# Gathering the experts' tokens from a split of the normalized rows, in fp32r instead of fp32

## The chip, the cores and the metric

One Trainium2 chip, one of its cores. The metric is the time of one execution on the device in microseconds (us). Four engines work in parallel: TensorE (in the profile PE for its products and PEld for its weight loads), VectorE (DVE), ScalarE (ACT) and GpSimd (POOL). SyncE (SP) issues most transfers.

## The reference, cut to what matters

Two layers of attention and feed-forward over 256 tokens of 1024 numbers, and a second block behind them. The part that the change touches is the feed-forward of the second layer, a mixture of 8 experts of which each token takes two:

```python
def moe_swiglu(h, router, wg, wu, wd):
    logits = (h @ router).astype(jnp.float32)
    top_vals, top_idx = lax.top_k(logits, TOP_K)
    gates = jax.nn.softmax(top_vals, axis=-1)
    ...
    for e in range(N_EXPERTS):
        out = out + gate_e[..., e:e + 1] * swiglu(h, wg[e], wu[e], wd[e])
```

`h` is the normalized input: x divided by its root mean square, times a gain per column. D is 1024, the inner width 3584, all in float32.

## The kernel before, in words

Products that need float32's precision are made in one of two ways. In plain fp32, TensorE takes both operands as they are. In fp32r, an operand is first split: ScalarE makes a rounded copy (the high part), VectorE subtracts it from the original (the low part), and three fp32r products (high by high, high by low, low by high) add up in PSUM. All expert weights go the second way: for each half of a unit of gate and up weights ScalarE copies (line 1675, `unit_high`) and VectorE subtracts (line 2256, `A_parts`, called by `unit_low`), and the same for the down weights (lines 1705 and 2336).

If no expert has more than 128 tokens, which is so here, each expert works on its own tokens alone. The steps for expert e:

- `one_hot` (line 2352) makes `sel`, 256 tokens by 128 slots, with a one where a token has a slot.
- `gather(e)` on TensorE (line 949) multiplies the normalized rows `xn` (the stationary operand, 128 tokens by 128 columns at a time) with `sel` (the moving operand, 128 slots wide): 8 blocks of columns by 2 blocks of tokens, 16 products in fp32. They go to the PSUM banks 6 and 7.
- `dispatch` on VectorE (line 2360) applies the gain and writes `xgT`; ScalarE (line 1725, `rows_part`) and VectorE (line 2371) split it into `xgs`.
- 14 units of 256 inner columns: gate and up products against `xgs` (line 894, two halves of 12 products), the gated hidden rows turned (line 909), split (ACT line 1685, DVE line 2317) and multiplied with the down weights (line 924, 12 products).
- `scatter` (line 962) puts the result back on the tokens, out of `ye`, a split of the expert's output whose low half lies in `hTR`.

The gather for expert e + 1 is issued by expert e after its unit 12 of 0 to 13, behind two turns of `selg` (line 975). Only the gather of expert 0 stands alone, ahead of all units. There is one buffer each for a half of the split gate and up weights and for the down weights, so VectorE's and ScalarE's work for one half waits until TensorE has used the half before. Every engine runs its own list in order; semaphores tie the lists. In expert 0, ScalarE runs `before(n)` at the start of unit n and VectorE runs `after(n)` at its end; GpSimd at the same time makes gate rows (lines 1486 to 1495) for the second block.

`hTR` is an fp32r buffer of 2048 columns whose storage is that of `hT`, the turned input of this and the earlier layers. In the expert branch it holds the low half of `ye`, and at the very end of the last expert the high part of one block of down weights.

Of the kernel before, what the change touches and what calls it, by code (L numbers as in the profile page):

```python
# [21 lines left out]
F32R = mybir.dt.float32r  # L22
I32 = mybir.dt.int32
U32 = mybir.dt.uint32
ALU = mybir.AluOpType
ACT = mybir.ActivationFunctionType
# [106 lines left out]
def build(nc, t, out, AT1, N1, AT2, N2):  # L133
    ctx = ExitStack()
    with ctx:
        def sb(name, shape, dt=F32):
            return ctx.enter_context(nc.sbuf_tensor(name, shape, dt))

        def sem(name):
            return ctx.enter_context(nc.semaphore(name))  # L140
# [7 lines left out]
        with nc.sbuf_tensor("hcTR", [P, KC, SEQ], F32R) as hcTR:  # L148
            pass
        hcT = sb("hcT", [P, KC, SEQ])  # L150
        xn = sb("xn", [P, TILES, D])
        with nc.sbuf_tensor("ringL", [P, 2, KC, BW], F32R) as ringL:
            pass
# [41 lines left out]
        As = sb("As", [P, 2, 2, KC // 2, BW], F32R)  # L195
        Bs = sb("Bs", [P, FB // P, 2, D], F32R)
        hds = sb("hds", [P, 2, 2, FB // P, P], F32R)
        f32 = lambda v: v.bitcast(F32)

        def ar(off, *shape):  # L200
            n = int(np.prod(shape))
            assert off + n <= AR_N, (off, n)
            v = arena[:, off:off + n]
            if len(shape) == 1:
                return v
            if len(shape) == 2:
                return v.rearrange("p (a b) -> p a b", a=shape[0])
            return v.rearrange("p (a b c) -> p a b c", a=shape[0], b=shape[1])
# [22 lines left out]
            return by_rows(xs[:, 0, :, :] if p["name"] == "ff0x" else hTR[:, :, :]), by_rows(ringH[:, b % 2, :, :])  # L231

        xgT = ar(0, KC, P)
        ye = arenaR[:, 1024:1024 + D], hTR[:, 0:4, :].rearrange("p k n -> p (k n)")
        sel = ar(2048, TILES, P)
        selg = ar(2304, TILES, P)
        selT = arenaR[:, 2560:2560 + TILES * P].rearrange("p (t s) -> p t s", t=TILES)
        chosen = ar(2816, TILES, NE)
# [93 lines left out]
        gates_open = sem("gates_open")  # L332
        y_mixed = sem("y_mixed")
        y_high = sem("y_high")
        xh_high, xh_low, z_first, i_lin, u_high, u_split = (sem(n) for n in ("xh_high", "xh_low", "z_first", "i_lin", "u_high", "u_split"))
        o_scaled, ot_tp, ot_hi, ot_lo = (sem(n) for n in ("o_scaled", "ot_tp", "ot_hi", "ot_lo"))
        wo_std, x_mixed, pn_plain, fin_std, x_out = (sem(n) for n in ("wo_std", "x_mixed", "pn_plain", "fin_std", "x_out"))
# [359 lines left out]
        def _(pe):  # L697
# [242 lines left out]
            def gather(e):  # L940

                pe.wait_ge(sel_ready, e + 1)
                if not isinstance(e, int) or e >= 2:
                    pe.wait_ge(added, 2 * e - 2)
                for half in range(2):
                    for k in range(4):
                        for tt in range(TILES):
                            o = (4 * half + k) * P
                            last = mm(ps[:, 6 + half, k * P:(k + 1) * P], xn[:, tt, o:o + P], sel[:, tt, :], start=tt == 0, stop=tt == TILES - 1)  # L949
                    last.then_inc(gathered, 1)  # L950

            def scatter(e, tt):
# [547 lines left out]
        def _(act):  # L1500
# [232 lines left out]
            def expert(e):  # L1733

                first, final = isinstance(e, int) and e == 0, isinstance(e, int) and e == NE - 1

                def before(n):
                    if n == 2 and not first:
                        keep_y(e - 1)

                def body(i, u, last):
                    if isinstance(i, int):
                        before(2 * i + u)
                    lead = first and isinstance(i, int) and i == 0
                    nxt = (i + 1, 0) if u else (i, 1)
                    if not lead:
                        part_high(e, i - 1, u, 1)
                    unit_high(e, *nxt, 0)
                    if last and not final:
                        rows_part(e + 1, 0)  # L1750
                    if u == 0:
                        gate_silu(e, i, 1)
                    unit_high(e, *nxt, 1)
                    if last and not final:
                        rows_part(e + 1, 1)
                    if last and final:
                        down_high(e, i, 0, down_home(ph["moe"], ph["moe"]["b"])[0], 0)
                        part_high(e, i, 0, 1)
                        part_high(e, i, 1, 1, 3)
                        down_high(e, i, 1, None, 2)  # L1760
                    elif u:
                        down_high(e, i, 0)
                    elif not lead:
                        down_high(e, i - 1, 1)
                blocks(act, NB1, body, 2)
                if final:
                    keep_y(e)
# [390 lines left out]
        def _(dve):  # L2158
# [214 lines left out]
            def expert(e):  # L2373

                first, final = isinstance(e, int) and e == 0, isinstance(e, int) and e == NE - 1

                def after(n):
                    if n in (2, 3) and not first:
                        add(e - 1, n - 2)
                    if n == 3:  # L2380
                        if not first:
                            dve.wait_ge(selg_tp, e)
                        one_hot(e, 2 * e + 2, True)
                        if not final:
                            dve.wait_ge(gathered, 2 * e + 2)
                            one_hot(e + 1, 2 * e + 3, False)
                    if n == NB1 - 2 and not final:
                        dispatch(e + 1)

                def body(i, u, last):  # L2390
                    lead = first and isinstance(i, int) and i == 0
                    nxt = (i + 1, 0) if u else (i, 1)
                    if isinstance(i, int) and i == 1 and u == 0 and not first:
                        y_low(e - 1)
                    if last:
                        gate_sums(e)
                    if not lead:
                        part_low(e, i - 1, u, 1)
                    unit_low(e, *nxt, 0)
                    if last and not final:  # L2400
                        rows_part(e + 1, 0)
                    if u:
                        gate_times_up(e, i, 1)
                    unit_low(e, *nxt, 1)
                    if last and not final:
                        rows_part(e + 1, 1)
                    if last and final:
                        down_low(e, i, 0, down_home(ph["moe"], ph["moe"]["b"]))
                        part_low(e, i, 0, 1)
                        part_low(e, i, 1, 1, 3)  # L2410
                        down_low(e, i, 1)
                    elif u:
                        down_low(e, i, 0)
                    elif not lead:
                        down_low(e, i - 1, 1)
                    if isinstance(i, int):
                        after(2 * i + u)
                blocks(dve, NB1, body, 2)
                if final:
                    y_low(e)  # L2420
                    dve.wait_ge(down_done, e * (2 * NB1) + (ph["moe"]["s"] + 2 * NB1))
# [615 lines left out]
```

## Time and profile before

| | |
|---|---|
| median of 3 runs | 2683.97 us (2683.48 to 2686.52) |
| the profiled execution | 2684.65 us |
| its span, first to last instruction | 2682.9 us |
| TensorE busy / weight loads busy | 2556.0 us (95%) / 2030.1 us (76%) |
| VectorE / ScalarE / GpSimd busy | 1819.1 (68%) / 1452.3 (54%) / 53.2 us (2%) |
| line 949, the gathers | 256 product records, 31.5 us busy |
| granted TensorE clock, mean | 0.972 of full speed |

The profiled execution is 1.75 us over its span and 0.7 us over the median of the runs. Product records overlap: each lasts from the entry of its first column to the end of its last, and the next one starts before that. What a product costs is therefore the distance between starts, and in a row that merges n of them it is the row's length, less one record's, divided by n - 1. A busy share near 100% says that products followed one another, not that the array worked at its peak.

### The profile page before, as it was taken

What the parts mean: (1) busy time and instruction counts of PE and PEld (TensorE: products, weight loads), DVE (VectorE), ACT (ScalarE), POOL (GpSimd) and SP (SyncE); (2) the same over time, 40 slices, a digit from 0 to 9 for tenths busy, and PEclk for the clock granted to TensorE, in tenths of its full rate; (3) what the DMA queues carried; (4) which work ended last, traced back from release to release, by engine and by line L of the source; (5) the groups of instructions that cost most, each with busy time, mean ns of one, the idle gap of its engine ahead of it and who ended that gap; (6) DMA issues with size and microseconds to landing.
All of it is one profiled execution on the core that took longest, in us unless ns stands there. A gap on an engine that the chain in (4) does not pass through costs nothing.

```text
span 2682.9 us, 33560 instructions
## 1 busy us (share of the span) xinstructions
PE 2556.0 (95%) x11949; PEld 2030.1 (76%) x11949; DVE 1819.1 (68%) x1778; ACT 1452.3 (54%) x1613; POOL 53.2 (2%) x40
## 2 busy tenths in 40 slices
PE   7899998888999999999999998999999999998998
PEld 6568887656878787878888886888884687776787
DVE  6554445548898988888888886545443475776544
ACT  4554434535677777777677675445432243466443
POOL 0000000016000000000000000000000000000000
PEclk9999998879999999999999998999999999999999
DMA  6865542749999999999999996556543343435552
GB/s 215 294 216 187 185 164 81 249 158 332 370 330 347 353 345 355 347 353 346 354 343 357 342 336 222 184 179 195 180 167 108 92 154 116 139 96 176 194 186 70
DMA packets 327743, 631.65 MB, mean 235 GB/s; under 512 B 14089, under 2 KB 112937, under 8 KB 327465
## 3 DMA queue, kind: packets, MB, share of 16 engines
q1 hardware_dynamic: 326792, 627.35, 67.4%
q0 software_dynamic: 864, 3.15, 0.3%
q8 instruction: 55, 0.90, 0.1%
q14 instruction: 32, 0.25, 0.0%
HBM read 629.40 MB, written 1.05 MB: 235 GB/s over the span
## 4 chain that ended last, share of the span: by engine, by line
PE 83%; DVE 8%; ACT 4%; issue 3%; DMA 1%; SPq 0%; DVEq 0%; ACTq 0%
PE ps L820 19%; PE ps L894 18%; PE ps L924 10%; PE ps L849 9%; PE ps L1285 6%; PE ps L754 5%; PE ps L1312 2%; DVE As L2256 2%; PE ps L1027 1%; PE ps L1217 1%; PE ps L949 1%; ACT As L1675 1%; PE ps L833 1%; PE ps L1276 1%; PE ps L909 1%
## 5 line engine op out<-in xcount | busy, mean ns | idle before, releaser
L2256 DVE TENSOR_TENSOR As<-ringA,As 128x2048 fp32r<-128x2048 f32 x318 | 735.8, 2316 | 224.5 <-ACT As L1594 129.5
L894 PE MATMUL ps<-As,xgs 128*128 128x512 f32 x2688 | 660.6, 395 | 9.8 <-DVE As L2256 6.7
L894 PEld LDWEIGHTS ps<-As,xgs 128*128 128x128 f32 x2688 | 494.8, 188 | 117.1 <-issue 7.1
L1675 ACT ACTIVATE As<-ringA 128x2048 fp32r<-128x2048 f32 x224 | 428.7, 1914 | 31.7 <-PE ps L894 30.2
L820 PE MATMUL ps<-As,xs 128*128 128x512 f32 x1632 | 392.4, 397 | 9.4 <-issue 5.4
L820 PEld LDWEIGHTS ps<-As,xs 128*128 128x128 f32 x1632 | 306.7, 190 | 76.1 <-issue 5.8
L924 PE MATMUL ps<-Bs,hds 128*128 128x512 f32 x1332 | 322.6, 391 | 10.5 <-DVE hds L2317 10.2
L924 PEld LDWEIGHTS ps<-Bs,hds 128*128 128x128 f32 x1332 | 248.6, 188 | 68.7 <-issue 15.2
L2336 DVE TENSOR_TENSOR Bs<-ringB,Bs 128x2048 fp32r<-128x2048 f32 x111 | 255.7, 2304 | 10.1 <-ACT Bs L1705 8.6
L1705 ACT ACTIVATE Bs<-ringB 128x2048 fp32r<-128x2048 f32 x111 | 213.1, 1920 | 69.9 <-PE ps L924 69.9
L849 PE MATMUL ps<-Bs,hds 128*128 128x512 f32 x1056 | 247.8, 390 | 0.0
L849 PEld LDWEIGHTS ps<-Bs,hds 128*128 128x128 f32 x1056 | 198.0, 188 | 41.9
L1594 ACT ACTIVATE As<-ringA 128x2048 fp32r<-128x2048 f32 x94 | 179.7, 1912 | 17.4 <-DMA ringA<-in_dense_w_up 10.1
L2300 DVE TENSOR_TENSOR Bs<-ringB,Bs 128x2048 fp32r<-128x2048 f32 x44 | 100.8, 2292 | 119.7 <-ACT Bs L1648 119.7
L1648 ACT ACTIVATE Bs<-ringB 128x2048 fp32r<-128x2048 f32 x44 | 84.3, 1916 | 135.4 <-PE ps L849 135.4
L2226 DVE TENSOR_TENSOR ringL<-ringA,ringH 128x2048 fp32r<-128x2048 f32 x42 | 96.1, 2290 | 57.4 <-ACT ringH L1574 57.1
L754 PE MATMUL ps<-As,xs 128*128 128x512 f32 (+1 forms) x384 | 119.0, 394 | 9.0 <-DVE ringL L2226 6.1
L1685 ACT ACTIVATE hds<-ps 128x256 fp32r<-128x256 f32 x112 | 43.1, 384 | 154.8 <-PE ps L909 153.6
L1615 ACT ACTIVATE hds<-ps 128x256 fp32r<-128x256 f32 x94 | 31.3, 382 | 170.8 <-PE ps L833 162.7
L1574 ACT ACTIVATE ringH<-ringA 128x2048 fp32r<-128x2048 f32 x42 | 80.1, 1910 | 79.2 <-PE ps L1285 57.7
L820 PE MATMUL ps<-As,hcTR 128*128 128x512 f32 x352 | 111.6, 398 | 0.0
L1636 ACT ACTIVATE sg<-ps 128x256 f32<-128x256 f32 x94 | 36.1, 385 | 126.8 <-PE ps L820 125.8
(380 smaller groups left out, 3214.6 us busy)
## 6 DMA issues: line engine op xcount, KB each, us to landing
ringA<-in_moe_w_gate SPq DMA_DIRECT2D x112, 1024.0 KB, 5.2
ringA<-in_moe_w_up SPq DMA_DIRECT2D x112, 1024.0 KB, 5.3
ringB<-in_moe_w_down SPq DMA_DIRECT2D x112, 1024.0 KB, 5.5
ringA<-in_w_ff_in SPq DMA_DIRECT2D x132, 512.0 KB, 4.8
ringA<-in_w_in SPq DMA_DIRECT2D x56, 1024.0 KB, 5.4
ringA<-in_w_ada SPq DMA_DIRECT2D x36, 1024.0 KB, 6.8
ringB<-in_w_ff_out SPq DMA_DIRECT2D x33, 1024.0 KB, 5.0
ringA<-in_dense_w_gate SPq DMA_DIRECT2D x28, 512.0 KB, 3.7
```

The source lines that it names most:

```text
L754: m = mm(ps[:, 4 + 2 * (n % 2) + tt, 0:cols], xs[:, l, k, tt * P:(tt + 1) * P], w, start=k == 0 and m_ == 0, stop=k == KC - 1 and m_ == 2)
L820: m = mm(ps[:, bank, :], lhs(l, tt, k), As[:, h, r, k % 4, :], start=k == 0 and n == 0, stop=k == KC - 1 and n == 2)
L849: m = mm(ps[:, 4 + 2 * tt + half, :], hds[:, buf, l, q, :], w[:, half * 512:(half + 1) * 512], start=first and q == 0 and n == 0, stop=q = ...
L894: m = mm(ps[:, bank, :], lhs(l, tt, k), As[:, h, r, k % 4, :], start=k == 0 and n == 0, stop=k == KC - 1 and n == 2)
L924: m = mm(ps[:, 4 + 2 * tt + half, :], hds[:, u if T == 1 else tt, l, q, :], (Bs[:, q, r, :] if weights is None else weights[r][:, q, :])[: ...
L1285: m = mm(dst, lhs[l][:, k, tt * P:(tt + 1) * P], w[q], start=k == 0 and m_ == 0, stop=k == KC - 1 and m_ == 2)
L1594: A(As[:, h, 0, :, :], ringA[:, (p["a"] + u) % 2, 4 * h:4 * h + 4, :], ACT.Copy).then_inc(A_high, 1)
L1675: A(As[:, h, 0, :, :], ringA[:, (p["a"] + u) % 2, 4 * h:4 * h + 4, :], ACT.Copy).then_inc(A_high, 1)
L1705: A(Bs[:, :, 0, :] if dst is None else dst, ringB[:, b0 % 2, :, :], ACT.Copy).then_inc(B_high, 1)
L2256: V.tensor_tensor(As[:, h, 1, :, :], ringA[:, (p["a"] + u) % 2, 4 * h:4 * h + 4, :], f32(As[:, h, 0, :, :]), ALU.subtract).then_inc(A_spli ...
L2300: V.tensor_tensor(Bs[:, :, 1, :], ringB[:, (p["b"] + u) % 2, :, :], f32(Bs[:, :, 0, :]), ALU.subtract).then_inc(B_low, 1)
L2336: V.tensor_tensor(lo, ringB[:, (p["b"] + u) % 2, :, :], f32(hi), ALU.subtract).then_inc(B_low, 1)
```

## The change

Once, during expert 0, the normalized rows are split. ScalarE writes a rounded copy of all of `xn` (128 by 2048) into `hTR`, at the start of unit 2, after the gather of expert 0 has read `xn`. VectorE subtracts it from `xn` in place, into `xnR`, an fp32r name of the same storage, at the end of unit 2. The gathers of experts 1 to 7 then make two fp32r products (high by `sel`, low by `sel`) for each one in fp32, so 32 products of 128 columns; `sel` is written in fp32r. The gather of expert 0 stays in fp32 and reads `sel` under its fp32 name. Since `hTR` is now taken for all of the experts, the low half of `ye` gets a buffer of its own, `yl`. Two semaphores are new.

```diff
+        with nc.sbuf_tensor("xnR", [P, TILES, D], F32R) as xnR:
+            pass
         xn = sb("xn", [P, TILES, D])
...
+        yl = sb("yl", [P, D], F32R)
...
-        ye = arenaR[:, 1024:1024 + D], hTR[:, 0:4, :].rearrange("p k n -> p (k n)")
-        sel = ar(2048, TILES, P)
+        ye = arenaR[:, 1024:1024 + D], yl[:, :]
+        x_split = hTR[:, :, :].rearrange("p k n -> p (k n)").rearrange("p (t n) -> p t n", t=TILES), xnR[:, :, :]
+        sel = arenaR[:, 2048:2048 + TILES * P].rearrange("p (t s) -> p t s", t=TILES)
...
+        xn_high, xn_split = sem("xn_high"), sem("xn_split")
... (TensorE, gather)
+                whole = isinstance(e, int) and e == 0
+                if not whole:
+                    pe.wait_ge(xn_split, 1)
                 for half in range(2):
                     for k in range(4):
+                        o = (4 * half + k) * P
                         for tt in range(TILES):
-                            o = (4 * half + k) * P
-                            last = mm(ps[:, 6 + half, k * P:(k + 1) * P], xn[:, tt, o:o + P], sel[:, tt, :], start=tt == 0, stop=tt == TILES - 1)
+                            if whole:
+                                last = mm(ps[:, 6 + half, k * P:(k + 1) * P], xn[:, tt, o:o + P], f32(sel[:, tt, :]), start=tt == 0, stop=tt == TILES - 1)
+                                continue
+                            for q in range(2):
+                                last = mm(ps[:, 6 + half, k * P:(k + 1) * P], x_split[q][:, tt, o:o + P], sel[:, tt, :], start=tt == 0 and q == 0, stop=tt == TILES - 1 and q == 1)
                     last.then_inc(gathered, 1)
... (ScalarE, expert, before(n))
+                    if n == 2 and first:
+                        act.wait_ge(gathered, 2)
+                        A(x_split[0], xn[:, :, :], ACT.Copy).then_inc(xn_high, 1)
... (VectorE, expert, after(n))
+                    if n == 2 and first:
+                        dve.wait_ge(xn_high, 1)
+                        V.tensor_tensor(x_split[1], xn[:, :, :], f32(x_split[0]), ALU.subtract).then_inc(xn_split, 1)
```

## Rows read from the trace of the kernel before

**Rows 1.** The page's first two parts: busy time, and the granted clock by slices.
```profile
PE 2556.0 (95%) x11949; PEld 2030.1 (76%) x11949; DVE 1819.1 (68%) x1778; ACT 1452.3 (54%) x1613; POOL 53.2 (2%) x40
...
PEclk9999998879999999999999998999999999999999
```

**Rows 2.** The page's chain of work that ended last, by engine.
```profile
PE 83%; DVE 8%; ACT 4%; issue 3%; DMA 1%; SPq 0%; DVEq 0%; ACTq 0%
```

**Rows 3.** The source line of the gathers: record durations in ns, and waits.
```profile
L949 PEld LDWEIGHTS ps<-arena,xn x256: 190/192/333, 605.6 to 1489.5; 128*128 128x128 f32 x128
L949 PE MATMUL ps<-arena,xn x256: 274/275/582, 605.6 to 1489.7; 128*128 128x128 f32 x128
its engine sat idle before it (us, times) until:
  DVE arena L2352: 8.5, 2
```

**Rows 4.** Timeline, all engines, around expert 1's gather: start, length, what, idle before.
```profile
728.33 0.38 PE L975 MATMUL ps<-c,arena 128*128 128x128 f32 x2
728.44 3.65 PEld L949 LDWEIGHTS ps<-arena,xn 128*128 128x128 f32 x32
728.55 3.74 PE L949 MATMUL ps<-arena,xn 128*128 128x128 f32 x32
728.59 1.91 ACT L1705 ACTIVATE Bs<-ringB 128x2048 fp32r<-128x2048 f32 x1 [0.34 <-PE ps L924]
730.53 2.29 DVE L2336 TENSOR_TENSOR Bs<-ringB,Bs 128x2048 fp32r<-128x2048 f32 x1
...
732.04 3.01 PE L894 MATMUL ps<-As,xgs 128*128 128x512 f32 x12
732.74 1.28 DVE L2360 TENSOR_TENSOR arena<-ps,vcol 128x512 f32<-128x512 f32 x2
...
740.60 2.93 PE L894 MATMUL ps<-As,xgs 128*128 128x512 f32 x12
```

**Rows 5.** Timeline of TensorE: narrow fp32 products, two or eight records a row.
```profile
500.11 0.39 PE L1077 MATMUL ps<-arena 128*128 128x64 f32 x2
500.33 0.39 PE L1078 MATMUL ps<-arena 128*128 128x64 f32 x2
500.56 0.39 PE L1079 MATMUL ps<-arena 128*128 128x64 f32 x2
...
504.85 1.05 PE L1009 MATMUL ps<-c,arow 128*128 128x2 f32 x8
```

**Rows 6.** Timeline of TensorE: fp32r products of 256 columns, first and last of 67.
```profile
2130.08 0.28 PE L1312 MATMUL ps<-hcTR,ringH 128*128 128x256 f32 x1
...
2138.00 0.28 PE L1312 MATMUL ps<-hcTR,ringH 128*128 128x256 f32 x1
```

**Rows 7.** Source lines: record durations, ns min/median/max.
```profile
L1009 PE MATMUL ps<-c,arow x96: 223/251/374, 83.3 to 541.9; 128*128 128x2 f32 x96
...
L1027 PEld LDWEIGHTS ps<-ringA,cT x288: 106/110/178, 74.8 to 595.0; 128*32 128x32 f32 x144
...
L894 PEld LDWEIGHTS ps<-As,xgs x2688: 186/188/192, 612.9 to 1616.9; 128*128 128x128 f32 x192
```

**Rows 8.** TensorE's groups of products by form: the fp32r lines' widths and means.
```profile
L894 PE MATMUL ps<-As,xgs 128*128 128x512 f32 x2688 | 660.6, 395 | 9.8 <-DVE As L2256 6.7 <-DVE xgs L2371 2.6
...
L1312 PE MATMUL ps<-hTR,ringH 128*128 128x256 f32 x192 | 55.1, 287 | 0.0
```

**Rows 9.** Stretches: length, busy PE, PEld, DVE, ACT, POOL (records), clock, DMA, GB/s.
```profile
644.89:675.00 30.11, 26.75 (x115) 20.82 (x115) 30.04 (x24) 18.48 (x13) 13.57 (x6) 1.00 0.99 369
675.00:728.30 53.30, 53.30 (x241) 43.78 (x240) 46.32 (x29) 40.09 (x29) 0.00 (x0) 1.00 1.02 379
728.30:744.00 15.70, 15.52 (x88) 13.06 (x86) 13.23 (x13) 9.06 (x8) 0.00 (x0) 1.00 0.78 281
...
857.90:874.00 16.10, 15.95 (x74) 12.73 (x73) 13.58 (x14) 9.75 (x10) 0.00 (x0) 1.00 0.78 269
```

**Rows 10.** Timeline, ACT, DVE and PE around expert 0's unit 2.
```profile
628.55 1.90 ACT L1705 ACTIVATE Bs<-ringB 128x2048 fp32r<-128x2048 f32 x1
...
631.37 0.39 ACT L1685 ACTIVATE hds<-ps 128x256 fp32r<-128x256 f32 x1 [0.92 <-issue]
631.65 1.91 ACT L1675 ACTIVATE As<-ringA 128x2048 fp32r<-128x2048 f32 x1
...
634.49 0.41 DVE L2317 TENSOR_TENSOR hds<-ps,hds 128x256 fp32r<-128x256 f32 x1
...
634.82 2.28 DVE L2256 TENSOR_TENSOR As<-ringA,As 128x2048 fp32r<-128x2048 f32 x1
...
641.44 3.12 DVE L2336 TENSOR_TENSOR Bs<-ringB,Bs 128x2048 fp32r<-128x2048 f32 x1
...
644.48 0.41 DVE L2317 TENSOR_TENSOR hds<-ps,hds 128x256 fp32r<-128x256 f32 x1
...
644.95 3.01 PE L924 MATMUL ps<-Bs,hds 128*128 128x512 f32 x12 [0.36 <-DVE hds L2317]
...
647.61 3.89 DVE L2256 TENSOR_TENSOR As<-ringA,As 128x2048 fp32r<-128x2048 f32 x1
```

**Rows 11.** The chain of work in 612 to 676 us, by line.
```profile
by line: DVE As L2256 43.2%; PE ps L894 25.0%; issue 12.0%; ACT As L1675 9.0%; DVE Bs L2336 3.6%; DVE hh L2329 2.0%; DVE xgs L2371 1.8%; PE ps L924 1.4%; DVE arena L2350 0.9%; DVE hds L2317 0.5%; DVE small L2346 0.3%; DVE small L2345 0.2%; 
```

## The prediction

> **What bounds the kernel now.** I read the page's busy shares first: TensorE is busy for 95% of the span at nearly the full clock, VectorE for 68% [rows 1], and the chain that ended last lies on TensorE for 83% of its length and on VectorE for 8% [rows 2]. The gathers are TensorE's work, so a shorter or longer gather should show in the total, unless VectorE stands right behind it. I therefore read three places. The first is the line of the gathers: 256 records for 8 gathers of 16 products, so a product in fp32 is two records, each with a weight load of its own [rows 3]. The second is the timeline of one gather in the middle of the run. There TensorE goes without a gap from the turns of `selg` into the gather and from it into the next unit [rows 4]; 32 records take 3.74 us, one lasts 0.275, so their starts are (3.74 - 0.275) / 31 = 0.112 us apart and a gather is 32 x 0.112 = 3.58 us of TensorE's time. The stretches around two such boundaries show TensorE idle for only 15.70 - 15.52 = 0.18 and 16.10 - 15.95 = 0.15 us [rows 9]. The third is expert 0, where the split is put. From 644.89 to 675.00 us VectorE is busy 30.04 of 30.11 us and TensorE idle 3.36; behind it, to 728.30, TensorE is never idle and VectorE has 7 of 53 us free [rows 9]. The chain through 612 to 676 us goes mostly over VectorE [rows 11]. So the gathers lie where TensorE sets the pace, and the new subtraction lies where VectorE does.
>
> **Part 1: the seven gathers of experts 1 to 7.** The records go from 32 with fp32 operands to 32 with fp32r operands. What sets 0.112 us? It could be the columns that pass, or the weight load ahead of each record. Narrower fp32 products answer it. With 64 columns instead of 128 the starts of three pairs are 500.11, 500.33 and 500.56, so 0.11 us per record; with 2 columns it is (1.05 - 0.25) / 7 = 0.114 [rows 5], one such record being 0.25 [rows 7]. Half the columns, or almost none, change nothing: below 128 columns the spacing is that of the loads of 128 weight columns. The loads' own records agree: 32 columns take 110 ns, 128 take 192 [rows 3, 7], so 0.85 ns per column and 109 ns for 128, the rest being latency.
>
> An fp32r product still loads 128 weight columns, and its load record is 188 ns [rows 7] against 192 for fp32 [rows 3], so I take it to be as long. The number of loads does not fall either: it was 2 per product for 16 products, it is 1 per product for 32. So 32 x 0.112 = 3.58 us against 3.58 us, and part 1 gives 0. The columns that pass may well halve, but they are hidden behind the loads.
>
> No row shows an fp32r product of under 256 columns: the narrowest are those of line 1312 [rows 8]. They start (2138.00 - 2130.08) / 66 = 0.120 us apart [rows 6]. From them come the bounds. Below: if the load did not count, half of 0.120 for half the columns, 0.060, so 32 x 0.060 = 1.92 us, 1.66 less per gather and 11.6 us less for seven. Close above: 0.120 as it stands, 32 x 0.008 = 0.26 us more per gather, 1.8 us for seven. Far above: if a product this narrow is carried out in the four passes of fp32, it is two records of 0.112, 32 x 0.224 = 7.17 us, 3.58 more per gather and 25.1 us for seven. I take 0, because the load's duration is the one thing that a row shows for both kinds. The added wait for `xn_split` was satisfied some 80 us before the first gather that asks for it: nothing.
>
> Two rules of the Trainium skill say otherwise. Its page FP8 and Floating Point Precision, section TensorE Precision Notes, has true fp32 as four passes through the array and the reduced kind as one of truncated values; by it a gather's passes fall from 64 to 32, and the sum would be the rival of the halved gather below. The rows agree on the passes of wide products and do not show them to count in narrow ones. Its page TensorE: Matmul & The Clock Gate, section Back-to-back issue gap, gives a stream of pairs of load and product with 128 columns some 81 ns each; by that figure seven gathers would shrink by 7 x 32 x 0.031 = 7 us, an estimate from that page. This trace shows no pair under 110 ns, which is why I do not use it.
>
> **Part 2: VectorE's subtraction, 128 by 2048, at the end of unit 2 of expert 0.** The same form costs 2.28 us on line 2256 undisturbed, and 3.89 when GpSimd works beside it [rows 10]. It goes in after line 2336 (641.44 + 3.12 = 644.56) and ahead of the split of the hidden rows at 644.48, for which TensorE already waits 0.36 us ahead of its down products at 644.95 [rows 10]. Behind the subtraction are that split, then both halves of the next unit's weights. VectorE has no free time up to 675 us in which to catch up [rows 9]. After it TensorE cannot make the lost time good, since it is never idle there. So it comes out of the end in full: +2.3 us. The bounds are 0 (if the wait is made good by work of GpSimd's that no longer falls on VectorE's) and 3.9 (if GpSimd slows it).
>
> **Part 3: ScalarE's copy, 128 by 2048, at the start of unit 2.** It costs 1.9 us, as line 1675 does. Its place is between 628.55 + 1.90 = 630.45 and the copy of the hidden rows at 631.37 [rows 10]: 0.92 us of it is free time. The hidden rows' copy and line 1675 move by 1.0 us, the latter to 631.65 + 1.0 + 1.91 = 634.56. VectorE comes to its subtraction for this copy at 634.82 anyway, and to the hidden rows at 634.49 [rows 10]. So the cover is VectorE's lag and the cost is 0, with 0.26 us to spare; without the cover it is up to 1.0 us. Its wait for the gather of expert 0 was met at 611 us.
>
> **Part 4: what moves.** The low half of `ye` in its own buffer and `sel` in fp32r leave the same instructions on VectorE with the same shapes: 0. No transfer is added or moved past a queue.
>
> **The sum** against the profiled execution's 2684.65 us is 0 + 2.3 + 0 + 0 = 2687.0 us. That execution is 0.7 us above the median of the runs, so the forecast for the median is 2683.97 + 2.3 = 2686.3 us, 0.09% more.
>
> **The rivals.**
>
> *A narrow fp32r product takes all four passes.* For it: this kernel has not one fp32r product under 256 columns, and nothing in the trace says that the single pass holds below that. Against it: the records of 512 and 256 columns last 395 and 287 ns [rows 8], in step with one pass of the columns, with no sign of a change on the way down. Time: seven gathers 25.1 longer, less the 0.15 to 0.18 us that TensorE idles at each boundary now (7 x 0.17 = 1.2), plus the split's 2.3: 2683.97 + 26.2 = 2710.2 us, slower by 1.0%. It decides as soon as the spacing passes 0.13 us: 7 x 32 x 0.014 = 3.1 us and the split together reach the 5.4 us that are 0.2%.
>
> *The gather is halved.* For it: half the passes. Against it: the loads. It needs an fp32r load of under 0.06 us, and the load's record gives no hint of that. VectorE also sets a limit: its instruction ahead of the dispatch ends at 730.53 + 2.29 = 732.82 whatever the gather does [rows 4], and the next expert's first products at 740.60 wait for rows that come from it. I allow 0.25 us lost per boundary. Time: 2683.97 - 11.6 + 1.8 + 2.3 = 2676.5 us, faster by 0.28%.
>
> *The split is hidden too, or costs double.* Same gathers, 2684.0 to 2689.7 us (3.9 for a slowed subtraction and 1.8 for a spacing of 0.120). The upper end is just past 0.2%.
>
> **How the numbers follow.** A measurement of this kernel tells about 0.2%, 5.4 us, from no change. The gather as long as before: 0.52, of which 0.03 lie above 2689.4. Four passes: 0.34, because nothing in the trace covers widths under 256 columns. Halved: 0.10. Something between the last two, or unforeseen: 0.04. The likeliest case is the first, 2686.3 us, its own range 2683.5 to 2690. To leave out no more than 2 in 10 the range must take in the case of four passes: 2681 to 2713 us; the halved gather falls outside. Chances: faster 0.11, within 0.2% 0.51, slower 0.38.
>
> **What would show it.** In the profile after, the gathers of experts 1 to 7 are 32 records each, on hTR and xn: if their starts are 0.11 us apart, part 1 holds; 0.06 is the halved gather; 64 records, or starts over 0.2 apart, the four passes. The product records should be shorter than 275 ns while the spacing stays, if the columns halve behind the loads. TensorE's first unit after the first gather should start 3.5 us after its start (now 728.55 to 732.04). In expert 0 TensorE should wait about 2.6 us for VectorE's line 2317 near 645 us, and be free of waits from about 677 us. The prediction is wrong if the weight load in fp32r is not what its record suggests, or if VectorE makes the 2.3 us good before 675.

## The result, and the profile after

| | before | after |
|---|---|---|
| median of 14 runs each | 2683.35 us (2679.23 to 2687.08) | 2690.98 us (2682.97 to 2696.61) |
| ratio, 95% interval | | 1.0026 (1.0018 to 1.0034) |
| profiled execution, span | 2682.9 us | 2688.9 us |

The changed kernel is slower by 0.26% by the ratio of all runs (7.0 us), just past the 0.2% that I had set as the bound of what can be told; the interval, 0.18 to 0.34%, reaches a little below that bound. The forecast was +2.3 us; it became +7.6 us in the medians and +6.0 in the two spans. The median lies in the stated range of 2681 to 2713 us, but above the 2683.5 to 2690 that I gave the likeliest case.

The page of the changed kernel, busy time and chain by engine, beside [rows 1, 2]:

```profile
PE 2556.0 (95%) x11949; PEld 2029.6 (75%) x11949; DVE 1823.0 (68%) x1779; ACT 1453.7 (54%) x1614; POOL 54.4 (2%) x40
...
PE 84%; DVE 7%; ACT 4%; issue 3%; DMA 1%; SPq 0%; DVEq 0%; ACTq 0%
```

TensorE is busy for the same 2556.0 us with the same 11949 records. So, summed over the whole execution, the 6.0 us of the spans are idle time of TensorE's and not longer products. VectorE has one instruction and 3.9 us more, ScalarE one instruction and 1.4 us more.

**The gathers.** The source line of the fp32r gathers, the half of its records with the high part (number, durations in ns min/median/max, first and last start), beside [rows 3]:

```profile
L961 PEld LDWEIGHTS ps<-arenaR,hTR x112: 190/192/192, 734.4 to 1495.3; 128*128 128x128 f32 x112
L961 PE MATMUL ps<-arenaR,hTR x112: 273/275/305, 734.4 to 1495.3; 128*128 128x128 f32 x112
```

And TensorE's timeline around the first of them (start, length, line, output<-inputs), beside [rows 4]:

```profile
734.39 0.30 PE L961 MATMUL ps<-arenaR,hTR 128*128 128x128 f32 x1
734.53 0.28 PE L961 MATMUL ps<-arenaR,xnR 128*128 128x128 f32 x1
...
737.88 0.27 PE L961 MATMUL ps<-arenaR,xnR 128*128 128x128 f32 x1
737.99 0.68 PE L899 MATMUL ps<-As,xgs 128*128 128x512 f32 x2
```

With as many for the low part, which last as long, these are 224 records, 32 for each of seven gathers. Their starts are (737.88 - 734.39) / 31 = 0.113 us apart, and the next unit's first product starts 3.60 us after the gather's, where before it was 732.04 - 728.55 = 3.49 [rows 4] (0.03 of the 0.11 more lies between the first two records). The loads last 192 ns as before. The product records last 275 ns too: they did not get shorter.

**Where the loss lies.** Stretches of the changed kernel: from the gather of expert 0 to that of expert 1, the last part of it, most of the six experts that follow, and two short stretches that come up below (columns as in [rows 9]):

```profile
604.75:734.39 129.64, 113.39 (x501) 91.46 (x501) 107.80 (x67) 80.33 (x58) 42.42 (x17) 0.96 0.91 328
...
677.00:734.30 57.30, 57.30 (x260) 47.00 (x259) 49.98 (x32) 42.59 (x32) 0.00 (x0) 1.00 1.01 369
760.00:1480.00 720.00, 710.96 (x3262) 581.33 (x3261) 638.55 (x457) 513.70 (x377) 0.00 (x0) 1.00 0.96 350
...
660.00:668.00 8.00, 5.86 (x18) 4.73 (x19) 6.37 (x6) 0.97 (x1) 5.00 (x2) 0.62 0.64 228
...
649.06:653.48 4.42, 3.40 (x15) 2.48 (x14) 4.42 (x4) 1.91 (x1) 0.61 (x1) 1.00 0.72 231
```

The same stretches of the kernel before, whose rows were not shown ahead of the prediction:

```profile
605.63:728.55 122.92, 112.29 (x501) 90.21 (x502) 104.97 (x66) 78.70 (x57) 41.26 (x17) 0.99 0.95 350
760.00:1480.00 720.00, 711.15 (x3261) 581.26 (x3260) 638.15 (x458) 513.26 (x377) 0.00 (x0) 1.00 0.96 350
...
649.94:657.50 7.56, 5.85 (x26) 4.31 (x25) 7.49 (x12) 4.63 (x5) 0.60 (x1) 1.00 1.04 393
```

Expert 0 takes 129.64 us instead of 122.92, which is 6.7 us more, for 501 product records in both. 5.6 of them are idle time of TensorE's (16.25 against 10.63) and 1.1 are longer products (113.39 against 112.29), at a mean clock of 0.96 against 0.99. Since the first gather starts 0.9 us earlier than before (604.75 against 605.63), 5.8 of the 6.7 reach the second gather's start (734.39 against 728.55), nearly all of the spans' 6.0. From 760 to 1480 us nothing differs, and from 677.00 on TensorE is busy without a break, so nothing that expert 0 lost is regained there. From the last gather's last record to the end of the span it is 1193.5 us after (2688.9 - 1495.4) and 1193.2 before (2682.9 - 1489.7).

**The chain of events in expert 0.** Timeline of the changed kernel, all engines, the rows that matter:

```profile
629.84 1.89 ACT L1754 ACTIVATE hTR<-xn 128x2048 fp32r<-128x2048 f32 x1
...
634.29 2.28 DVE L2271 TENSOR_TENSOR As<-ringA,As 128x2048 fp32r<-128x2048 f32 x1
...
643.95 2.28 DVE L2395 TENSOR_TENSOR xnR<-xn,hTR 128x2048 fp32r<-128x2048 f32 x1
...
645.99 2.49 POOL L1507 TENSOR_TENSOR gateG<-gateG,arow 128x1024 f32<-128x1024 f32 x1 [2.37 <-DMA arow<-in_norm_g]
646.15 0.41 DVE L2332 TENSOR_TENSOR hds<-ps,hds 128x256 fp32r<-128x256 f32 x1
646.48 4.13 DVE L2271 TENSOR_TENSOR As<-ringA,As 128x2048 fp32r<-128x2048 f32 x1
...
646.62 3.04 PE L929 MATMUL ps<-Bs,hds 128*128 128x512 f32 x12 [2.57 <-DVE hds L2332]
649.06 0.61 POOL L1498 DMA_DIRECT2D arow<-in_b_ada  x1 [0.59 <-POOL gateG L1507]
...
653.48 4.37 POOL L1501 TENSOR_TENSOR gateG<-gateG,arow 128x1024 f32<-128x1024 f32 x1 [3.81 <-DMA arow<-in_b_ada]
...
655.54 2.33 DVE L2360 COPY small<-slots 128x2 f32<-128x2 f32 x1
...
657.98 1.90 DVE L2365 TENSOR_SCALAR arena<-c,small 128x128 f32<-128x128 f32 x2
...
658.74 2.78 POOL L1504 TENSOR_SCALAR gateG<-gateG 128x1024 f32<-128x1024 f32 x1
659.80 0.16 DVE L2360 COPY small<-slots 128x2 f32<-128x2 f32 x1
...
660.06 1.61 DVE L2367 TENSOR_SCALAR arenaR<-c,small 128x128 fp32r<-128x128 f32 x2
661.60 0.41 DVE L2332 TENSOR_TENSOR hds<-ps,hds 128x256 fp32r<-128x256 f32 x1
...
662.14 4.80 PE L929 MATMUL ps<-Bs,hds 128*128 128x512 f32 x12 [5.46 <-DVE hds L2332]
666.77 2.89 PE L899 MATMUL ps<-As,xgs 128*128 128x512 f32 x12
```

The one-hots of unit 3 of the kernel before, its timeline, for comparison:

```profile
649.94 0.60 POOL L1486 DMA_DIRECT2D arow<-in_b_ada  x1 [0.59 <-POOL gateG L1495]
...
653.63 0.15 DVE L2345 COPY small<-slots 128x2 f32<-128x2 f32 x1
...
653.89 0.60 DVE L2350 TENSOR_SCALAR arena<-c,small 128x128 f32<-128x128 f32 x2
...
655.07 0.42 DVE L2317 TENSOR_TENSOR hds<-ps,hds 128x256 fp32r<-128x256 f32 x1
...
655.62 3.01 PE L924 MATMUL ps<-Bs,hds 128*128 128x512 f32 x12 [1.05 <-DVE hds L2317]
657.53 2.42 POOL L1489 TENSOR_TENSOR gateG<-gateG,arow 128x1024 f32<-128x1024 f32 x1 [6.98 <-DMA arow<-in_b_ada]
```

The reader is to see three things in the changed kernel. The subtraction takes 2.28 us and starts right behind the down weights; the hidden rows' split comes 2.2 us after it, and TensorE waits 2.57 us. That is the forecast. Then come the eight small instructions that make the one-hots (`selg` and `sel`, two copies and two comparisons each). From the first of them at 655.54 to the hidden rows' split behind them at 661.60 it is 6.06 us, where before it was 655.07 - 653.63 = 1.44. The first of them copies 128 by 2 numbers, needs 0.15 us before and takes 2.33 here: it starts inside GpSimd's addition and ends at 657.87, with it (653.48 + 4.37 = 657.85). The two pairs of comparisons are stretched from 0.60 and 0.48 to 1.90 and 1.61. Last, TensorE waits 5.46 us for the hidden rows behind them (1.05 before), and the 12 products after that wait take 666.77 - 662.14 = 4.63 us of TensorE's time instead of some 2.85 (655.62 to 658.47 before). In the stretch around them, 660 to 668 us, the granted clock is 0.62 on average, between the full 2.4 GHz and the lower level of 1.2.

Counted from the first gather, the hidden rows of unit 3 are split 56.85 us after it instead of 49.44, so 7.4 later: 0.35 from ahead of the subtraction, 2.2 the subtraction, 0.24 between, 4.6 the one-hots. The 0.35 are not from ScalarE's copy: the first products of expert 0 are late by as much (612.43 - 604.75 = 7.68 against 612.96 - 605.63 = 7.33 before). The slow products bring it to 9.2. By the next gather it is 6.7: TensorE waits no more from 666.77 us on, where before it still had three waits for VectorE, 1.6 us in all of the 2.5 regained.

### The profile page after: what moved, and what is told of

It is laid out like the page before. It is cut to its first block, busy times and chain, and to the rows that moved or that the text cites. A ratio compares the mean times of both kernels' runs of the same rounds, so it can differ in the third digit from the quotient of the medians.

```text
span 2688.9 us, 33569 instructions
## 1 busy us (share of the span) xinstructions
PE 2556.0 (95%) x11949; PEld 2029.6 (75%) x11949; DVE 1823.0 (68%) x1779; ACT 1453.7 (54%) x1614; POOL 54.4 (2%) x40
## 3 DMA queue, kind: packets, MB, share of 16 engines
HBM read 629.40 MB, written 1.05 MB: 234 GB/s over the span
## 4 chain that ended last, share of the span: by engine, by line
PE 84%; DVE 7%; ACT 4%; issue 3%; DMA 1%; SPq 0%; DVEq 0%; ACTq 0%
PE ps L825 19%; PE ps L899 18%; PE ps L929 10%; PE ps L854 9%; PE ps L1297 6%; PE ps L759 5%; PE ps L1324 2%; DVE As L2271 2%; PE ps L1039 1%; PE ps L1229 1%; PE ps L961 1%; ACT As L1687 1%; PE ps L838 1%; PE ps L914 1%; PE ps L1288 1%
## 5 line engine op out<-in xcount | busy, mean ns | idle before, releaser
L2351 DVE TENSOR_TENSOR Bs<-ringB,Bs 128x2048 fp32r<-128x2048 f32 x111 | 255.0, 2297 | 12.8 <-ACT Bs L1717 11.3
```

The source lines that it names most:

```text
L2351: V.tensor_tensor(lo, ringB[:, (p["b"] + u) % 2, :, :], f32(hi), ALU.subtract).then_inc(B_low, 1)
```

## The experiments

Gather 0 and gather 1 below are the first starts of the gathers of experts 0 and 1; the one-hots' time is from the first small copy of unit 3 to the hidden rows' split. All are from one profiled execution each. Expert 0 does not start at the same time in all of them, and where it starts early (e2, e5) it is also longer, so both columns have to be read, the start of gather 1 and the distance.

| kernel | subtraction | gather 0 | gather 1 | apart | one-hots |
|---|---|---|---|---|---|
| before | none | 605.63 | 728.55 | 122.9 | 1.44 |
| after | unit 2 | 604.75 | 734.39 | 129.6 | 6.06 |
| e1 | unit 2 | 605.89 | 735.20 | 129.3 | 3.16 |
| e4 | unit 2 | 604.15 | 733.80 | 129.7 | 6.06 |
| e9 | unit 2 | 604.75 | 734.27 | 129.5 | 6.05 |
| e10 | unit 2 | 604.63 | 734.37 | 129.7 | 6.06 |
| e3 | unit 3, after the one-hots | 604.53 | 732.59 | 128.1 | 1.4 (and 2.2 the subtraction) |
| e6 | unit 8 | 604.04 | 728.88 | 124.8 | 1.44 |
| e5 | units 5 to 8, in quarters | 597.86 | 727.39 | 129.5 | 6.05 |
| e2 | none | 599.78 | 729.19 | 129.4 | 1.44 |
| e7 | none, GpSimd later | 601.58 | 717.53 | 116.0 | 1.46 |
| e8 | unit 2, GpSimd later | 599.98 | 717.34 | 117.4 | 1.45 |
| e11 | none, GpSimd later | 605.35 | 721.21 | 115.9 | 1.45 |
| e12 | unit 2, GpSimd later | 599.30 | 716.51 | 117.2 | 1.45 |

| kernel | median us (runs) | before, same chip | ratio (95%) |
|---|---|---|---|
| e1 | 2687.83 (9) | 2681.98 (27) | 1.0024 (1.0014 to 1.0034) |
| e2 | 2681.28 (11) | 2681.98 | 0.9995 (0.9985 to 1.0004) |
| e3 | 2687.43 (12) | 2681.98 | 1.0015 (1.0004 to 1.0025) |
| e4 | 2675.04 (6) | 2681.98 | 0.9973 (0.9961 to 0.9984) |
| e5 | 2684.99 (12) | 2683.58 (34) | 1.0004 (0.9995 to 1.0012) |
| e6 | 2687.06 (12) | 2683.58 | 1.0013 (1.0003 to 1.0024) |
| e7 | 2681.20 (12) | 2683.58 | 0.9990 (0.9981 to 0.9999) |
| e8 | 2677.74 (11) | 2683.58 | 0.9984 (0.9971 to 0.9996) |
| e9 | 2690.78 (1) | 2683.23 (19) | a single run |
| e10 | 2690.58 (1) | 2683.23 | a single run |
| e11 | 2674.13 (8) | 2683.23 | 0.9965 (0.9954 to 0.9976) |
| e12 | 2675.93 (12) | 2683.23 | 0.9975 (0.9966 to 0.9984) |

The ratio is taken over all runs and not from the two medians, so the two can differ by a microsecond or two: e3 is 5.5 us over in the medians and 4.0 by its ratio.

### The split without the fp32r gathers (e1)

The gathers are fp32 again and read the high part alone; the low part is left out.

```diff
-for q in range(2):
-    last = mm(ps[...], x_split[q][:, tt, o:o + P], sel[:, tt, :], start=tt == 0 and q == 0, stop=tt == TILES - 1 and q == 1)
+last = mm(ps[...], f32(x_split[0][:, tt, o:o + P]), f32(sel[:, tt, :]), start=tt == 0, stop=tt == TILES - 1)
```

> The split as in the changed kernel, but the gathers of experts 1 to 7 are 16 fp32 products again, read from the rounded high part alone (the low part is left out of the result). Theory 1 (the whole loss is the split in expert 0; 32 narrow fp32r products cost what 32 fp32 records did): as slow as the changed kernel, some 2690 us, 6 to 7 us over before. Rival (part of the loss is in the fp32r gathers): between before and the changed kernel, under 2687 us.

Timeline of this kernel, expert 0 and the first fp32 gather:

```profile
654.27 4.52 DVE L2350 TENSOR_TENSOR Bs<-ringB,Bs 128x2048 fp32r<-128x2048 f32 x1
658.72 0.99 DVE L2359 COPY small<-slots 128x2 f32<-128x2 f32 x1
...
662.43 5.24 PE L929 MATMUL ps<-Bs,hds 128*128 128x512 f32 x12 [4.82 <-DVE hds L2331]
...
735.20 3.74 PE L960 MATMUL ps<-arenaR,hTR 128*128 128x128 f32 x32
```

The ratio is that of the change, and gather 1 is as late. So, within the intervals, the whole loss comes with the split and none with the gathers. Here GpSimd's addition meets the down weights' subtraction (4.52 us instead of 2.28) and then its multiplication two of the small copies (0.99 and 1.04).

### The gathers and the copy without the subtraction (e2)

```diff
-pe.wait_ge(xn_split, 1)
+pe.wait_ge(xn_high, 1)
...
-last = mm(..., x_split[q][:, tt, o:o + P], sel[:, tt, :], ...)
+last = mm(..., x_split[0][:, tt, o:o + P], sel[:, tt, :], ...)
...
-if n == 2 and first:
-    dve.wait_ge(xn_high, 1)
-    V.tensor_tensor(x_split[1], xn[:, :, :], f32(x_split[0]), ALU.subtract).then_inc(xn_split, 1)
```

> The fp32r gathers with 32 narrow products and ScalarE's copy stay; VectorE's subtraction is gone, and both products of a pair read the high part (the low part is left out and the high one counts twice). Theory 1: the time of before, 2683 us, with 0.112 us between the gathers' starts, ScalarE's copy hidden. Rival (the copy or the gathers cost): 2686 us or more.

The time is that of before within the interval (4.0 us less to 1.1 more). 32 fp32r products for a gather and ScalarE's copy cost nothing that these runs can tell: the loss is VectorE's one instruction and what follows from it. The low part is left out here, and the high one counts twice. The profiled expert 0 of this run is 129.4 us long without any subtraction, but it began 6 us early, its one-hots took 1.44 us, and it reaches gather 1 at 729.19, as before; this is taken up under what stays open.

### Half the products (e4)

```diff
-for q in range(2):
-    last = mm(ps[...], x_split[q][:, tt, o:o + P], sel[:, tt, :], start=tt == 0 and q == 0, stop=tt == TILES - 1 and q == 1)
+last = mm(ps[...], x_split[0][:, tt, o:o + P], sel[:, tt, :], start=tt == 0, stop=tt == TILES - 1)
```

> As the changed kernel, but the gathers of experts 1 to 7 make only the high product of each pair, 16 fp32r products (the low part is left out). Theory 2 (a record costs its weight load, 0.112 us, whatever passes): each gather 16 x 0.112 = 1.8 us shorter, 12.5 us less for seven, 10 to 12 us under the changed kernel after what VectorE takes back at the boundaries. Rival (the boundaries are set by VectorE, and a shorter gather only turns into a wait): under 5 us less.

Timeline of TensorE at the first of these gathers:

```profile
733.80 1.98 PE L960 MATMUL ps<-arenaR,hTR 128*128 128x128 f32 x16
735.62 1.60 PE L899 MATMUL ps<-As,xgs 128*128 128x512 f32 x6
```

(1.98 - 0.275) / 15 = 0.114 us a record, and the next unit starts 1.82 us after the gather instead of 3.60. It is 12.8 us under e1, which has the same split and ran on the same chip; 7 x 16 x 0.112 = 12.5. So the gathers lie wholly on the path, and what counts there is the number of records. Had fp32r halved a record's time, as one rival has it, about as much would have come off the changed kernel's time.

### 64 and 256 columns in each product (e9, e10)

```diff
-last = mm(ps[:, 6 + half, k * P:(k + 1) * P], x_split[q][:, tt, o:o + P], sel[:, tt, :], ...)
+last = mm(ps[:, 6 + half, k * P:k * P + 64], x_split[q][:, tt, o:o + P], sel[:, tt, 0:64], ...)                       # e9
+last = mm(ps[:, 6 + half, (k // 2) * SEQ:(k // 2 + 1) * SEQ], x_split[q][:, tt, o:o + P], sel[...] as 256 columns, ...)  # e10
```

> As the changed kernel, but in the gathers of experts 1 to 7 each fp32r product takes only the first 64 slots of the selection (the other half of the gathered rows is left as it was). Theory 2 (the load of 128 weight columns sets the pace of a narrow fp32r product): starts 0.112 us apart as with 128 columns. Rival (the columns that pass set it): about 0.06 us apart.

> As the changed kernel, but in the gathers of experts 1 to 7 each fp32r product takes 256 columns, both tiles of the selection side by side, and two blocks share one place in PSUM (the gathered rows are a mixture). Theory 2: starts 0.12 us apart, as in the second block's products of 256 columns, so twice the columns for 7% more time. Rival (the columns set it): 0.22 us apart.

With 64 columns, the products of the high part by the source line, and the first and the last product of the first gather in the timeline:

```profile
L961 PE MATMUL ps<-arenaR,hTR x112: 276/277/339, 734.3 to 1496.7; 128*128 128x64 f32 x112
...
734.27 0.28 PE L961 MATMUL ps<-arenaR,hTR 128*128 128x64 f32 x1
...
737.78 0.40 PE L961 MATMUL ps<-arenaR,xnR 128*128 128x64 f32 x1
```

The same with 256:

```profile
L961 PE MATMUL ps<-arenaR,hTR x112: 279/281/366, 734.4 to 1497.0; 128*128 128x256 f32 x112
...
734.37 0.37 PE L961 MATMUL ps<-arenaR,hTR 128*128 128x256 f32 x1
...
738.13 0.28 PE L961 MATMUL ps<-arenaR,xnR 128*128 128x256 f32 x1
```

(737.78 - 734.27) / 31 = 0.113 us and (738.13 - 734.37) / 31 = 0.121. The loads last 192 and 188 ns. Half the columns change nothing and twice the columns add 7%. One run each gave 2690.78 and 2690.58 us; the changed kernel's median is 2690.98. So from 64 to 128 columns it is not the columns that set the pace but what a record costs besides, its weight load among it, and 256 columns cover that nearly evenly. That it is the load itself, and not some fixed cost of a record, is argued from the length of the load records ahead of the prediction; no run had products this narrow with fewer than 128 weight columns.

### The subtraction behind the one-hots (e3)

```diff
-(at the end of n == 2)
+(at the end of n == 3, after one_hot(e + 1, 2 * e + 3, False))
 dve.wait_ge(xn_high, 1)
 V.tensor_tensor(x_split[1], xn[:, :, :], f32(x_split[0]), ALU.subtract).then_inc(xn_split, 1)
```

> The subtraction moves from the end of unit 2 to the end of unit 3, behind the small one-hot instructions of that unit, which then keep their place between GpSimd's. Theory 1a (some 4 of the 6 us came because the late one-hots met GpSimd's addition and were held up, and TensorE's clock fell in the long wait): 2 to 3.5 us over before. Rival 1b (any 2.3 us of VectorE's work added in this phase costs 6): 6 us over before again. The long wait of TensorE for VectorE near 660 us should be about 3 us, not 5.5.

Timeline, VectorE and TensorE:

```profile
654.38 2.29 DVE L2404 TENSOR_TENSOR xnR<-xn,hTR 128x2048 fp32r<-128x2048 f32 x1
...
657.14 3.00 PE L929 MATMUL ps<-Bs,hds 128*128 128x512 f32 x12 [3.25 <-DVE hds L2332]
...
668.97 4.59 PE L929 MATMUL ps<-Bs,hds 128*128 128x512 f32 x12 [1.79 <-DVE hds L2332]
```

The one-hots, from 652.94, escape (0.16 us the first copy), as the order was meant to make them. But in this execution the loss is only moved: TensorE waits 1.79 us more a unit later, and those products again run at a low clock (4.59 us for 12). That wait follows a subtraction for the down weights that took 4.48 us beside GpSimd, at 664.02. The ratio, 1.0015, lies between the two theories, its interval (1.1 to 6.7 us) takes in both, and the median, 2687.43, is not to be told from e1's 2687.83. So e3 doesn't show that the one-hots alone make the excess.

### The split later: in quarters, or whole in unit 8 (e5, e6)

```diff
-if n == 2 and first:
+if 5 <= n <= 8 and first:        # e5: one quarter of 512 columns each; e6: if n == 8 and first:
...
-pe.wait_ge(xn_split, 1)
+pe.wait_ge(xn_split, 4)          # e5 only
...
-blocks(dve, NB1, body, 2)
+blocks(dve, NB1, body, 5 if first else 2)   # ScalarE's the same
```

> The split in four pieces of 128 by 512, one in each of the units 5 to 8 of expert 0, where GpSimd has finished and TensorE sets the pace; VectorE and ScalarE have units 0 to 9 of expert 0 written out for it. Theory 1 (the loss is where VectorE sets the pace): each 0.68 us fits into VectorE's free 1.1 us per unit, so the time of before, within 1 us. Rival (VectorE's free time cannot be used, since the single buffers tie it to TensorE): 2 to 3 us over before.

> The split in one piece in unit 8 of expert 0 (VectorE and ScalarE have units 0 to 9 written out). Theory 1: 2.3 us at once are more than the slack of one unit, so TensorE waits once, 0.5 to 1.5 us, and the time is 0.5 to 1.5 us over before, far under the changed kernel. Rival (a subtraction costs its full length or more wherever it stands): 2.3 us or more over before.

The quarters' source line in e5, and a row of the timeline of its unit 3, where no part of the split has run yet:

```profile
L2398 DVE TENSOR_TENSOR xnR<-xn,hTR x4: 684/684/685, 672.6 to 697.9; 128x512 fp32r<-128x512 f32 x4
...
647.62 2.33 DVE L2362 COPY small<-slots 128x2 f32<-128x2 f32 x1
```

The timeline of e6, TensorE behind the subtraction at 697.83:

```profile
700.58 3.01 PE L929 MATMUL ps<-Bs,hds 128*128 128x512 f32 x12 [1.17 <-DVE hds L2332]
```

In quarters the split is not to be told from nothing (1.0004). Whole, past GpSimd's work, it makes TensorE wait 1.17 us, and the profiled expert 0 is 1.9 us longer than before's. The median says +3.5, with an interval from 0.8 to 6.4 us; the profile accounts for about half of that. So the wait is the one that was expected, while the time is nearer to the rival's 2.3 us or more, which this experiment does not rule out. And e5 shows that the collision of one-hots and GpSimd needs no split: its expert 0 started 8 us early, its one-hots met GpSimd by themselves, and TensorE waited 5.44 us behind them.

### GpSimd's work moved behind the experts (e7, e8, e11, e12)

```diff
 pool.wait_ge(spread_copied, units_before(NADA))
+pool.wait_ge(x_ready, XR["moe"])                     # e7 on the kernel before, e8 on the changed one
+pool.wait_ge(down_done, ph["ff0c"]["s"] + 2 * 3)     # e11 on the kernel before, e12 on the changed one
```

> The kernel before with one wait added on GpSimd: its gate rows are made after the last expert instead of during expert 0. Theory 3 (GpSimd holds up VectorE in expert 0): VectorE's subtractions there take 2.3 us instead of up to 3.9, TensorE idles less between 613 and 675 us, and the time is 3 to 7 us under before. Rival (TensorE's waits there come from the pipeline's filling, and GpSimd's rows are then late or disturb the next phase): no change, or slower.

> The changed kernel with GpSimd's gate rows made after the last expert. Theory 1a and 3 (the extra 4 us are the meeting of the one-hots with GpSimd, and without it the subtraction costs at most its own 2.3 us): at most 2.3 us over the kernel before with the same wait, and at or under before. Rival 1b (the loss has nothing to do with GpSimd): again 6 us over the kernel before with the same wait.

> The kernel before, with GpSimd's gate rows made from the third unit of the feed-forward behind the experts on, where VectorE is half idle, not at its very start. Theory 3 (expert 0 gets 6 to 7 us shorter without GpSimd; with the rows right behind the experts part of it was lost again in the final normalization): 5 to 8 us under before. Rival (GpSimd disturbs VectorE as much there and TensorE waits for it): no more than the 2 to 4 us of the wait placed at the experts' end.

> The changed kernel with GpSimd's gate rows in the same place. Theory 1a: the split costs what its subtraction does, 1 to 2.5 us over the kernel before with the same placement. Rival 1b: 6 us over it.

The wait of e7 and e8 holds GpSimd's gate rows back until the last expert is done, that of e11 and e12 until the third unit of the feed-forward behind it. The timeline of e12, the changed kernel with GpSimd idle in expert 0:

```profile
636.75 0.50 PE L929 MATMUL ps<-Bs,hds 128*128 128x512 f32 x1 [0.94 <-DVE hds L2333]
...
644.03 0.16 DVE L2361 COPY small<-slots 128x2 f32<-128x2 f32 x1
```

Stretches of e11 behind the experts:

```profile
1640.00:1800.00 160.00, 160.00 (x722) 131.71 (x721) 92.13 (x82) 74.03 (x84) 41.02 (x18) 0.99 0.58 192
```

With GpSimd away from it, expert 0 is 7.1 us shorter without the split (e11, 115.9) and 12.4 shorter with it (e12, 117.2), and e7 and e8 give nearly the same (116.0 and 117.4). The split then lengthens the profiled expert 0 by 1.4 us in both pairs, instead of 6.7. The medians do not resolve so little: e12 is 1.8 us over e11, e8 is 3.5 us under e7, and in both pairs the intervals overlap. They do say that the 7.6 us are gone. In the profiles e8 and e12 also begin expert 0 earlier than e7 and e11, by 1.6 and 6.0 us, which no run explains.

At the first later place (e7) the 7 us came back behind the experts: from the last gather's last record to the end it took 1200.3 us against 1193.2 (1195.5 in e8), and the median is only 2.4 us under before, less than the 3 to 7 expected. At the second place GpSimd's 41 us lie in a stretch in which TensorE is busy 160.00 of 160.00 us and VectorE only 92. e11, the kernel before with one more wait, has the lowest median of the versions that leave nothing out: 0.35% under before, 9.1 us, a little more than the 5 to 8 expected. Its profiled execution, 2681.07 us, was the longest of its eight, with 1958.1 us from gather 1 to the end against before's 1954.4 and e12's 1953.2; where it lost these four was not followed up.

## Why the prediction was right in its parts and short in its sum

**Part 1 (0) held.** The columns do not set the pace: it is 0.113 us a record for 64 and 128 of them, 0.121 for 256. From gather 1's start to the last record of the last gather it is 761.0 us (734.39 to 1495.4), before 761.2 (728.55 to 1489.7). Neither four passes (64 records or 0.224 us) nor a halved gather appeared, and e2 finds no cost in the median. One guess about what would show it failed: the product records did not shorten. A record of 64, 128 or 256 columns lasts 277, 275 and 281 ns, so the length of a short record says nothing of its columns; the distance between starts does.

**Part 3 (0) held.** The copy runs at 629.84, the hidden rows' copy follows, and VectorE's subtraction for the next weights comes at 634.29 without a wait; the 0.35 us by which expert 0 is late there were lost before the copy.

**Part 2 (+2.3) is the term that was mis-sized.** The direct part came as written: 2.28 us, a wait of 2.57 us at 646.62 where I had said 2.6 near 645, and no wait from 677 us. What failed is the sentence of the bounds, "0 (if the wait is made good by work of GpSimd's that no longer falls on VectorE's) and 3.9 (if GpSimd slows it)". It asks what GpSimd does to the subtraction and not what it does to the instructions that the subtraction pushes back. The one-hots ended at 655.07 and GpSimd's addition began 2.5 us later in the trace of before, at 657.53; a delay of 2.3 us brings the two to touching, which the rows of before could have told. I had treated everything behind the subtraction as a fixed length moved to the right. It cost 4.6 us more, and behind the wait of 5.46 us the 12 products took 1.8 us more at a granted clock of 0.62. In the five profiled executions with the subtraction in unit 2 and GpSimd's work in its old place (after, e1, e4, e9, e10), gather 1 starts at 733.80 to 735.20 us; in the four of before, e2, e5 and e6 it starts at 727.39 to 729.19.

The other half of the collision is not from the delay: by that alone the two would just have missed each other. GpSimd asks for its input 44.31 us after gather 0 in both kernels (649.94 before, 649.06 after), but its addition starts 7.6 us later before and 4.4 after. In between the DMA engines are busy 1.04 and 0.72 of the time, and in e1 0.69 with the addition 4.3 us after the request; in e3 and e5, where no subtraction runs ahead of the request, it is 6.2 and 5.9 us at 1.03. That fits weights asked for later, because VectorE frees their buffers later, and GpSimd's transfer gaining by it; this was not tested alone.

The Trainium skill has the rule that I did not weigh. Its page SBUF — State Buffer, section Who interferes with whom, has VectorE in its two-port modes and GpSimd take turns at a shared pair of ports, the later one blocked until the other's instruction ends. By the same section a VectorE instruction with two inputs in SBUF contends with a GpSimd instruction that reads SBUF. The trace agrees for the copy at 655.54, which ends with GpSimd's addition, though no view shows which mode it ran in, and for the two-input subtraction at 646.48, which takes 4.13 us, 2.13 of it after GpSimd's instruction ends at 648.48, about as long as it takes alone. It does not agree for the copy at 659.80, which takes 0.16 us inside GpSimd's multiplication of 658.74 to 661.52, nor for a pair of comparisons in e1 that takes its 0.60 us inside one of 657.53 to 661.42. That GpSimd's work in expert 0 makes the excess is shown by e8 and e12; that the ports are the way it does is argued.

**The chances.** 0.38 for slower stood mostly on the four passes, which no run shows. It came out slower by another way, which I had only as the double cost at 2689.7 us. That the range holds the measured time is luck in this sense: it reached up to 2713 us for the sake of the four passes, and the case that came true, the first one, had its own range end at 2690.

**What stays open.** How often the collision happens over many executions isn't measured, only that all five profiles with the subtraction in unit 2 and GpSimd in its old place have it, and that e5 has it too, with no subtraction ahead of it and hardly a loss in its runs (1.0004). e3 and e6 cost 4.0 and 3.5 us by their ratios, some 2 us and 1 us more than the subtraction's 2.3, but both intervals take in the 2.3; the profile of e3 shows where more could come from, that of e6 does not. And e2 and e5 begin expert 0 some 6 to 8 us earlier than before does but reach gather 1 hardly sooner (729.19 and 727.39 against 728.55); in e2 TensorE's products are 4.2 us longer there than before's, at a mean granted clock of 0.94 against 0.99, and why wasn't settled.

## What to carry to other kernels

Here narrow fp32 and fp32r products cost the same 0.11 us a record, each with its weight load, whatever passes up to 128 columns: count the records, and compare the distance between starts, before hoping for fewer passes. An instruction added to a saturated engine costs its own length and whatever the instructions behind it newly meet, so lay the other engines' timeline, GpSimd's first, under the shifted one. And where two engines collide, the work of the idle one may be worth more moved than the change itself: one wait on GpSimd gave 0.35%.

## What the runs showed of the hardware that I had not expected

- A VectorE copy of 128 by 2 numbers, 0.15 us alone, took 2.33 us and ended with the GpSimd addition beside it (e5: 2.33 as well; 0.99 in e1). Comparisons of 128 by 128, 0.60 and 0.48 us a pair alone, took 1.90 and 1.61 behind it; in e1 a pair took 0.60 beside a GpSimd multiplication. What decides was not settled.
- Behind a wait of TensorE's of 5.46 us, 12 products of 512 columns took 4.80 us instead of 2.88 to 3.04, the mean granted clock from 660 to 668 us being 0.62. Behind the wait of 2.57 us they took 3.04. In e1 it was 5.24 us behind 4.82, and in e3 4.59 behind only 1.79, that one following waits of 3.25 and 0.98 us.
- fp32r products, each with a load of 128 weight columns, start 0.113 us apart with 64 and with 128 columns, and 0.121 with 256.
